# A two-layer block on one core: the norm behind the feed-forward part worked out from three sums, and the convolution's first two blocks multiplied together

## The reference, cut to what matters

```python
def rmsnorm(x, g):
    return x * rsqrt(mean(x * x, -1) + EPS) * g
# first block, its end: 512 tokens, 1024 channels
h = rmsnorm(x, g_ff_pre)
y = square(relu(h @ w_ff1)) @ w_ff2              # 1024 -> 4096 -> 1024
x = x + rmsnorm(y, g_ff_post)
# second block, layer 0
mod = silu(c) @ ada_w + ada_b                    # 1024 -> 6144 per layer, two layers
sh1, sc1, g1, sh2, sc2, g2 = split(mod, 6)
h = rms_norm(x, norm1_g) * (1 + sc1) + sh1
a, gate = split(h @ conv_w_in, 2)
u = a * sigmoid(gate)
y = depthwise_conv(u, 31 taps) + dw_b
y = silu(layer_norm(y)) @ conv_w_out
x = x + g1 * y                                   # then the mlp, the second layer and a last norm
```

## Time and profile before

| | us |
|---|---|
| median of three runs | 2109.14 |
| the profiled execution: its own time | 2108.77 |
| its span, first to last instruction | 2107.0 |
| TensorE busy | 2060.1 (98%) |
| VectorE busy | 1242.7 (59%) |
| ScalarE busy | 833.4 (40%) |
| GpSimd busy | 211.5 (10%) |
| mean granted TensorE clock | 0.996 |

### The profile page before, as it was taken

One profiled execution on the slowest core, in us unless ns is written; L12 is line 12 of the kernel. 1 busy time (PEld: TensorE's weight loads), 2 busy tenths in 40 slices (PEclk: granted clock), 3 DMA queues, 4 the chain that ended last, 5 costly groups with the idle time before them and its releaser, 6 DMA issues.

```text
span 2107.0 us, 27557 instructions
## 1 busy us (share of the span) xinstructions
PE 2060.1 (98%) x11212; PEld 1669.2 (79%) x11212; DVE 1242.7 (59%) x1951; ACT 833.4 (40%) x1362; POOL 211.5 (10%) x182
## 2 busy tenths in 40 slices
PE   8999999999999999999999999999999989999998
PEld 7787877678878886666988888888887779888887
DVE  5565746446677777986644344476776756343443
ACT  5345544445323233225423233355464544232232
POOL 1321011011000004553000000100000010000002
PEclk9999999999999999999999999999999999999999
DMA  6313422125677772662242233221222232323331
GB/s 205 113 56 94 153 86 81 39 61 202 237 266 246 262 251 95 163 176 81 82 139 91 92 100 98 71 66 49 70 72 60 81 97 84 114 89 98 100 101 40
DMA packets 219710, 245.56 MB, mean 117 GB/s; under 512 B 9272, under 2 KB 205368, under 8 KB 213440
## 3 DMA queue, kind: packets, MB, share of 16 engines
q1 hardware_dynamic: 209360, 231.20, 33.9%
q10 hardware_dynamic: 10224, 12.61, 2.4%
HBM read 237.75 MB, written 3.78 MB: 115 GB/s over the span
## 4 chain that ended last, share of the span: by engine, by line
PE 87%; DVE 5%; ACT 4%; DMA 3%; issue 1%; ACTq 0%; POOL 0%; DVEq 0%; SPq 0%
PE bank L1438 24%; PE bank L1442 23%; PE bank L1446 23%; PE bank L1464 2%; PE bank L1472 2%; PE bank L1468 2%; DMA raw<-in_hgrn_in 1%; PE bank L1574 1%; DVE wL L2066 1%; PE bank L1624 1%; PE bank L1532 1%; PE bank L1509 1%; ACT wH L1692 1%; PE bank L1517 1%; PE bank L1557 1%
## 5 line engine op out<-in xcount | busy, mean ns | idle before, releaser
L1438 PE MATMUL bank<-hH,wH 128*128 128x512 f32 (+1 forms) x1768 | 644.4, 385 | 22.2 <-ACT wH L1697 7.9
L1442 PE MATMUL bank<-hH,wL 128*128 128x512 f32 (+1 forms) x1768 | 626.8, 375 | 0.0
L1446 PE MATMUL bank<-hL,wH 128*128 128x512 f32 (+1 forms) x1768 | 626.8, 375 | 0.0
L1692 ACT ACTIVATE wH<-raw 128x1024 fp32r<-128x1024 f32 (+1 forms) x376 | 333.7, 937 | 375.2 <-PE bank L1446 289.1
L2066 DVE TENSOR_TENSOR wL<-raw,wH 128x1024 fp32r<-128x1024 f32 (+1 forms) x340 | 377.9, 1149 | 131.4 <-ACT wH L1692 131.3
L1438 PEld LDWEIGHTS bank<-hH,wH 128*128 128x128 f32 x1768 | 326.6, 189 | 106.2 <-issue 34.2
L1446 PEld LDWEIGHTS bank<-hL,wH 128*128 128x128 f32 x1768 | 326.8, 189 | 61.0 <-DVE hL L2086 0.3
L1442 PEld LDWEIGHTS bank<-hH,wL 128*128 128x128 f32 x1768 | 327.4, 189 | 59.0 <-issue 2.2
L1438 PE MATMUL bank<-hidH,wH 128*128 128x512 f32 (+1 forms) x800 | 305.1, 381 | 1.9 <-ACT hidH L1856 1.9
L1446 PE MATMUL bank<-hidL,wH 128*128 128x512 f32 (+1 forms) x800 | 304.6, 381 | 0.0
L1442 PE MATMUL bank<-hidH,wL 128*128 128x512 f32 (+1 forms) x800 | 304.4, 381 | 0.0
(11 more groups left out here) (224 smaller groups left out, 2026.0 us busy)
## 6 DMA issues: line engine op xcount, KB each, us to landing
raw<-in_mlp SPq DMA_DIRECT2D x64, 1024.0 KB, 5.3
araw<-in_ada_w SPq DMA_DIRECT2D x48, 1024.0 KB, 5.2
raw<-in_w_ff SPq DMA_DIRECT2D x32, 1024.0 KB, 7.3
raw<-in_hgrn_in SPq DMA_DIRECT2D x32, 512.0 KB, 3.8
raw<-in_w_in SPq DMA_DIRECT2D x11, 1024.0 KB, 5.3
raw<-in_conv_in SPq DMA_DIRECT2D x16, 512.0 KB, 4.0
u<-conv_u ACTq DMA_DIRECT2D x24, 270.0 KB, 5.1
raw<-in_w_mv SPq DMA_DIRECT2D x4, 1024.0 KB, 5.2
```

What stands on the lines that cost most here:

```text
L1438: mm(out, wH[:, s, m:m + 128], xh[:, k, c], start=k == 0, stop=False)
L1442: mm(out, wL[:, s, m:m + 128], xh[:, k, c], start=False, stop=False)
L1446: i = mm(out, wH[:, s, m:m + 128], xl[:, k, c], start=False, stop=k == KB - 1)
L1692: do(wH[:, s, c], raw[:, r, c], ACT.Copy).then_inc(*s_whi.up(n, x))
```

## The change

1. `post_pre(..., None, ...)`, `square_mm` and `mod_norm` go. With r the root for y, q the sum of (g y)^2 and p the sum of x g y, the new x has the sum of squares sum(x^2) + r (2 p + r q). The first sum is kept from the norm before the feed-forward part (`xsq`, one ScalarE copy). In round 3 each block of y also gets `cross` on VectorE (a product, and an add into `psum`) and `gsq` on ScalarE (a square, added into `qsum` by GpSimd). `join` sums the three with two ones matmuls each, then ScalarE makes the root twice, VectorE does five operations in a row on one tile, and ScalarE a logarithm and an exponential.
2. `post` and `post_x` move behind the join: two blocks ahead of `mod`, then in turn with `mod` and `mod_lo`. `post` now writes to SBUF for all blocks, and GpSimd adds blocks 1, 3, 5, 7.
3. The pieces of blocks 0 and 1 become one pair of 256 columns, all four products in turn (`both`, 96 matmuls); their low parts are VectorE's. `conv_pe` of 0 and of 1 both stand behind the products of block 2.
4. VectorE's taps: of block b it does `AHEAD[b]` in the round of its u and the rest after u of the next block; the whole 15 of block 0 come before u of block 2. For block 6 that is 9 and 6, and the six stand behind u of block 7.
5. `RM` is 0.62, so the last `ada` item comes at step 205 of 244, before round 3 of w_ff2. `join` reads `araw`, which has to be free by then.

```diff
-BY_POOL = (0, 2, 4, 5)
+BY_POOL = (1, 3, 5, 7)
+AHEAD = (0, 0, 2, 4, 6, 8, 9, 3)
-RW, RM = 1.87, 0.52
+RW, RM = 1.87, 0.62
+JOIN_BUSY = 6
@@ post_pre, mod_norm -> join_part, join
+    def join_part(self, j):
+        for kind, key in (("cross", ("dve", "cross")), ("gsq", ("act", "gsq"))):
+            s, free = self.tmps.get() if j else (None, ())
+            self.do(kind, j=j, s=s, free=free)
...
+    def join(self):
...
+        for j in range(2):
+            post(j)
+            add(j)
+        for j in range(KB):
+            s, free = self.tmps.get()
+            self.do("mod", tag="c1", j=j, s=s, half=None, after=(*free, self.x_event("ff_post", j)))
+            post(j + 2)
+            self.do("mod_lo", tag="c1", j=j, s=s, half=None)
+            self.tmps.put(s, ("lo", "c1", j))
+            add(j + 2)
...
@@ both
-            ns = [self.take("conv_in", 0, c, 128, ahead=c == 0) for c in (0, 1024)]
+            ns = [self.take("conv_in", 0, c, 256, ahead=c == 0) for c in (0, 1024)]
@@ the loop over blocks
+        frees = [diagonal(blk) for blk in range(2)]
+        both()
+        for blk in range(2):
+            copies(blk, frees[blk])
+        taps_dve(0, range(conv_first(0)))
+        for blk in range(2, KB):
...
+            for j in (0, 1) if blk == 2 else (blk - 1,):
+                sums[j] = taps_pe(j)
+            copies(blk, diagonal(blk))
...
+            if blk == 2:
+                conv_sum(0, sums[0])
+            taps_dve(blk - 1, range(AHEAD[blk - 1], conv_first(blk - 1)))
+            conv_sum(blk - 1, sums[blk - 1])
+            taps_dve(blk, range(AHEAD[blk]))
@@ tensor_program, join
+                    mm(by, ones, nacc[:], start=True, stop=False)
+                    mm(bp, ones, psum, start=True, stop=False)
+                    mm(by, ones, tmp[:, it["ty"], :], start=False, stop=True).then_inc(*s_mm.up("join", "y"))
+                    mm(bq, ones, qsum, start=True, stop=False)
+                    mm(bq, ones, tmp[:, it["tq"], :], start=False, stop=True).then_inc(*s_mm.up("join", "q"))
+                    mm(bp, ones, tmp[:, it["tp"], :], start=False, stop=True).then_inc(*s_mm.up("join", "p"))
@@ vector_program, join
+                    e.tensor_tensor(w, banks[it["bq"]][:], w, MUL).then_inc(*s_dve.up("join", 0))
+                    e.scalar_tensor_tensor(out=w, in0=banks[it["bp"]][:], scalar=2.0, in1=w, op0=MUL, op1=ADD).then_inc(
+                    e.tensor_tensor(w, root, w, MUL).then_inc(*s_dve.up("join", 2))
+                    e.tensor_tensor(w, w, xsq[:], ADD).then_inc(*s_dve.up("join", 3))
+                    e.tensor_scalar(w, w, 0.0, None, MAX).then_inc(*s_dve.up("join", 4))
```

More of the change, by code:

```diff
@@ L374, in close @@
     def close(self, tag, size, busy=0, out=None):
[L376 to L385, removed]
+        b, after = self.lin.get()
+        total, tail, key = self.acc, self.tail, ("mm", "sum", tag)
+        self.tail = None
+        if tail is not None:
+            self.tmps.put(tail[0], key)
         self.do("close", tag=tag, size=size, b=b, after=after, total=total, tail=tail, key=key, rstd_free=self.rstd_free,
                 out=out, half=None)
-        self.lin.put(b, ("act", "ln", tag))
+        self.lin.put(b, ("act", "xsq" if tag == "ff_pre" else "ln", tag))
         self.acc, self.nsq = (key,), 0
@@ L515, in post_pre @@
     def post_pre(self, tag, nxt, src):
[L517 to L550, removed]
@@ new lines, in post_pre @@
+        self.close(tag, 1024, busy=BUSY)
+        add = {}
+        for j in range(KB):
+            self.do("post", tag=tag, src=src, j=j, rb=None, z=None)
+            if j:
+                self.do("pre_lo", tag=tag, nxt=nxt, j=j - 1)
+            self.do("post_x", tag=tag, src=src, j=j, pool=False, z=None)
+            self.do("pre_hi", tag=tag, nxt=nxt, j=j)
+            if j < 4:
+                self.to_add = None
+                self.square(nxt, j, ("xT", j), (self.x_event(tag, j),), by="dve")
+                add[j + 2], self.to_add = self.to_add, None
+            if add.get(j) is not None:
+                self.do("add_square", **add[j])
@@ L551, in post_pre, with rest @@
+        self.do("pre_lo", tag=tag, nxt=nxt, j=KB - 1)
+        def rest():
+            for j in range(4, KB):
+                self.square(nxt, j, ("xT", j), (self.x_event(tag, j),))
+        self.beside = rest
         self.rstd_free = (("dve", "post", tag, KB - 1),)
@@ L895, in both, with copies @@
             for n in ns:
-                self.piece_done[n] = parts[1]["key"]
-            for p, ev in zip(parts, (to_a, to_u(0))):
+                self.piece_done[n] = parts[-1]["key"]
+            for p, ev in zip(parts, (to_a, to_u(0), to_a, to_u(1))):
                 self.lin.put(p["b"], *ev(p["key"][1], 0, p["b"]))
             self.highs(ns[1] + NSPLIT)
-            do("shift_first", blk=0, slot=slots[0], after=())
             self.lows()
+        def copies(blk, free):
+            if direct(blk):
+                do("shift_first", blk=blk, slot=slots[blk], after=free)
+            else:
+                do("park", blk=blk)
+            do("shift", blk=blk, slot=slots[blk], after=free)
         mu = {}
@@ L1307, in build_program @@
         yr = mstrip
+        psum, qsum = araw[:, 0, 0:T], araw[:, 0, T:2 * T]
         memx = [qk[:, 8 + j, :].rearrange("p (b t) -> p b t", b=2) for j in range(4)]
```

178 lines of the change are left out of this document (124 added, 54 removed).

## The result

The changed kernel takes 2123.67 us (median of 4 runs, 2121.41 to 2129.06) beside 2110.02 us for the kernel before (4 runs, 2108.25 to 2112.22): a ratio of 1.0068, interval 1.0056 to 1.0080. It is slower by some 14 us, where I forecast no measurable change (2109.4) and a range up to 2116. The profiled execution took 2121.41 us, span 2119.6, as against 2108.77 and 2107.0, so 12.6 us are to be placed. I cut the span at rows that both kernels have: the first product of w_ff1, the end of the last w_ff2 product, the first convolution product, the end of the 96 products of blocks 0 and 1, u of block 7, the first conv_out product.

What follows compares the result with a forecast made beforehand. TensorE was taken as the bound, 87% of the chain that ended last. Terms -8.5 + 0.8 - 0.8 + 0.4 + 2.9 + 3.7 + 2.1 = +0.6 on 2108.77 gave 2109.4 us; own range 2106 to 2113, with rivals 2103 to 2116.

Steps and rivals of the forecast that it cites:

- Part 5: Feed-forward stage, faster `ada`: +2.1 us, of which 1.0 for a sum moved into TensorE's stream, 1.1 for VectorE's lag; range 0 to 7.
- the 821: End of the feed-forward stage: the prediction called itself wrong if the stage ended after 821 us.
- the lag's term: Ends of rounds 1 and 2: TensorE waits some 1.4 us twice in place of 1.6 once, +1.1 us.
- Rival B: Feed-forward stage: `araw` loads set VectorE's pace, TensorE waits 6 us at one round's end or the other; 2115.4 us, chance 0.17.
- Part 1: Seam from last w_ff2 product to first convolution product: 20.8 us become 12.3, 8.5 gained; bounds 7.5 to 9.5.
- Part 2: Modulation beside blocks 0 and 1's products: GpSimd's adds block VectorE, +0.8 us, half of 1.8 left after cover; range 0 to 2.
- Part 3: Convolution order: new TensorE waits of 0.4 and 2.9 us for copies of blocks 0 and 1, 0.8 of old ones gone.
- the 0.8 that goes: Convolution: TensorE's old 0.63 us wait for block 0's copies, with what surrounds it, disappears: -0.8 us.
- Part 4: Convolution's tail: six taps of block 6 ahead of block 7's sum, 4.7 us less 1.0 slack: +3.7; bounds 2.7 and 4.8.
- A: Faster: convolution copies land in time and the feed-forward lag stays under 2.8 us; 2104.2 us, chance 0.22.
- C: Modulation: the shared lock makes VectorE the bound, full 5.0 us without cover, +4.2 more; 2113.6 us, chance 0.07.
- D: Seam not shortened: a wait in the join costs what the five steps save, +8.5; 2117.9 us, chance 0.01.

Runs made afterwards that it cites:

- e2_pace_late_sum: Kernel before with RM 0.62 in place of 0.52 and each `ada` sum three empty steps later in the side list: 2118.98 us, ratio 1.0043.

## Why the prediction was wrong

**Part 5, +2.1 against +14.4, is the step that failed**, far beyond its own range of 0 to 7; the stage ended at 828.5 us, behind the 821 that I had named as a sign of being wrong. It failed in two places: the lag's term of 1.1 us, which measured 8.1 in waits alone, and what I put at nothing. The first is where the lag is paid. I gave VectorE 2.8 us of slack and charged TensorE's waits at the hidden tile only. The sum is a second meeting point, and I costed it as 1.00 us of matmuls without asking what it waits for. It was hit 4 times for 9.1 us, the longest time in round 3's w_ff1, where I had written that `ada` is over. The second is its size. My rate was right: 3.8 + 3.0 us a block, 6.8 measured. But I followed the list to a lag of 4.1 us at the two round ends, and with the sums out of the way e2_pace_late_sum shows 5.01 and 3.07 us of waiting above the slack of 2.8: 7.8 and 5.9. I relied on pauses in the list to fall just where I needed them. I also left out what comes after a wait, the slower clock, and priced the bank of `xsq` at nothing because ScalarE was waiting, though TensorE waited for ScalarE there; it measured 1.1.

The 1.36 us between relu and low part stood in my own row, and I added it to VectorE's 3.8 us as if it were work. It was idle time inside an in-order queue, a third of the block's own cost, and the part that an edit could take away. Rival B had the right engine and stage, but it had the lag come out at the round ends, its 6 us are less than half of what the stage lost beyond the forecast (12.3), its time of 2115.4 is 8.3 short, and its cause was wrong: leaving the loads out changed next to nothing.

**Part 1** held: -9.3 against -8.5, within 7.5 to 9.5, the join's five steps 832.93 to 836.4.

**Part 2**, +0.8 against +2.1. The subtraction beside a GpSimd add of 1.30 us took 1.79 where its neighbours took 0.75, so each of the three adds that met one cost 1.04 us. I had halved the rule's 1.8, hoping that the adds would fall beside `post`, and they did not. The rule of the Trainium skill ("SBUF — State Buffer", "Who interferes with whom") taken at its hardest was nearer than my half of it. The sum of the parts would have been 1 us higher by it, too little to change the outcome.

**Part 3**, +2.5 against +4.3: block 1's copies were late by 2.76 us (forecast 2.9); block 0's not at all (0.4). What I missed is again the clock: the taps behind that wait took 5.34 us in place of 3.64. With the 0.8 that goes this makes 3.7; the other 0.6 isn't placed. In the six other runs of this order the wait was 4.2 to 4.8 us, so the nearness of 2.76 to the forecast was luck of the profiled run.

**Part 4** held: +3.3 against +3.7. But the sum of block 7 came at 975.3, not within 4 us of 961.3, as everything ahead of it was late.

Of the other rivals, A had asked for the opposite in part 5; C's price was half there, without deciding anything; D did not come about.

## What to carry to other kernels

Follow side work that shares an in-order engine to every place where the bounding engine meets it, a little sum in its own queue as well as the big tiles, and price the lag at the first of them. A wait between two operations of one engine (here relu, two ScalarE steps, low part) costs little while the engine has slack and is the first thing to fill when its load goes up: one product of each block moved into it gave back 11 us. And give the kernel before each gain that does not need the change: the filled wait with the faster rate reached 2107.37 us without the join, and 2106.70 with the join and the later taps. Parts of a change can need one another, as the join needs the faster rate here: undo one part alone before calling it the culprit.

## What the runs showed of the hardware

After the 3.86 us without a matmul that ended at 772.76, the granted clock from 772 to 776 us was 0.57, near the lower of its two levels (1.2 of 2.4 GHz), and 1.00 from 776 to 780; the sum and the first three products took 1.5 us more than at full clock. Around and after the 2.76 us that ended at 881.47 it was 0.81 (878 to 884 us) and 0.91 (884 to 890), and the 32 matmuls of block 1's taps took 1.7 us more. Even the 1.93 us wait for the copy of `xsq`, ended at 485.45, is followed by eight products 0.43 us apart (0.68 from 484 to 489 us). The profile's idle column shows nothing of this.

The lock of part 2 shows in round 3 too: the add to `psum` (L2265), two SBUF tiles of 128 x 512, took 1.68 to 1.75 us each of the six times, always beside a GpSimd add, where the same form alone (L2301) took 0.68. No wait of TensorE came of it there.
